# A warm-up on a tile that VectorE writes, and the first norm's weight column on GpSimd's queue

## The reference

```python
def rmsnorm(x, w):
    xf = x.astype(jnp.float32)
    y = xf * lax.rsqrt(jnp.mean(xf * xf, axis=-1, keepdims=True) + EPS)
    return (y * w.astype(jnp.float32)).astype(x.dtype)

h = rmsnorm(x, norm_mix_w[l])
proj = h @ w_in                      # 1024 -> hq, hf, hi, hgate, gq, gk, gv, ggate, glr
f = lb + (1.0 - lb) * jax.nn.sigmoid(hf.astype(f32))
...
x = x + token_mix(...)               # two gated recurrences and an output projection
x = x + cross_attend(...)            # attention into 256 memory tokens
x = x + moe(...)                     # top 4 of 32 experts, clamped SwiGLU
return rmsnorm(x, norm_final_w)
```

## Time and profile before

| what | value |
|---|---|
| median of 3 runs | 1188.06 us (1187.84 to 1188.17) |
| profiled execution | 1188.46 us |
| its span, from first to last instruction | 1186.7 us |
| TensorE busy | 1137.7 us, 96% of the span |
| VectorE, ScalarE, GpSimd busy | 32%, 15%, 2% |
| mean transfer rate | 375 GB/s, 444.89 MB |
| chain that ended last | PE 68%, DMA 30%, DVE 1% |

### The profile page before, as it was taken

The page is one execution under the profiler, slowest core; times in us unless marked ns, Lnnn a source line. Parts: engine busy times, 40 slices in busy tenths (PEclk is TensorE's granted clock), DMA queues, the critical chain, the costliest instruction groups (busy, mean ns, idle before and its releaser), DMA issues.

```text
span 1186.7 us, 18637 instructions
## 1 busy us (share of the span) xinstructions
PE 1137.7 (96%) x7483; PEld 572.1 (48%) x7484; DVE 379.4 (32%) x896; ACT 175.2 (15%) x366; POOL 19.0 (2%) x58
## 2 busy tenths in 40 slices
PE   9999999999999999999999999999999999999997
PEld 5988879855443443334333333333333333333332
DVE  4688878545222111122212121111111111111112
ACT  5311421243100000001000000000000000000002
POOL 3000010000000000000000000000000000000000
PEclk9999999999999999999999999999999999999999
DMA  9954203989999999999999999999999999999995
GB/s 306 380 196 144 73 10 120 350 334 383 420 426 434 430 429 432 426 436 429 435 430 430 435 428 436 430 434 430 433 432 429 436 428 436 429 434 423 426 424 222
DMA packets 42853, 444.89 MB, mean 375 GB/s; under 512 B 6308, under 2 KB 6772, under 8 KB 26040
## 3 DMA queue, kind: packets, MB, share of 16 engines
q1 hardware_dynamic: 41912, 441.63, 88.9%
q0 software_dynamic: 480, 1.85, 0.7%
q10 hardware_dynamic: 416, 0.79, 0.2%
HBM read 443.20 MB, written 1.05 MB: 374 GB/s over the span
## 4 chain that ended last, share of the span: by engine, by line
PE 68%; DMA 30%; DVE 1%; ACT 0%; SPq 0%; issue 0%; DVEq 0%; ACTq 0%
DMA ring<-in_w_gate_up 30%; PE bank L1168 23%; PE bank L1159 13%; PE bank L733 7%; PE bank L729 4%; PE bank L1198 4%; PE bank L1213 3%; PE bank L712 2%; PE bank L873 1%; PE bank L1095 1%; PE bank L1284 1%; PE bank L1189 1%; PE bank L1275 1%; PE bank L1007 1%; PE bank L1129 1%; PE bank L1087 1%
## 5 line engine op out<-in xcount | busy, mean ns | idle before, releaser
L1168 PE MATMUL bank<-ring,region 128*64 128x512 f32 x2048 | 464.2, 608 | 36.4 <-DMA ring<-in_w_gate_up 36.4
L1168 PEld LDWEIGHTS bank<-ring,region 128*64 128x64 f32 x2048 | 147.1, 140 | 333.9 <-issue 268.6
L1159 PE MATMUL bank<-ring,region 128*64 128x512 f32 x1024 | 226.8, 596 | 0.3 <-ACT region L1407 0.3
L2290 DVE TENSOR_SCALAR region<-bank 128x512 f32<-128x512 f32 x32 | 22.1, 692 | 570.4 <-PE bank L1168 570.4
L1159 PEld LDWEIGHTS bank<-ring,region 128*64 128x64 f32 x1024 | 71.2, 137 | 130.0 <-issue 127.2
L1407 ACT ACTIVATE region<-bank 128x256 f32<-128x256 f32 (+1 forms) x134 | 55.4, 440 | 369.0 <-PE bank L1159 251.0
L733 PE MATMUL bank<-ring 128*128 128x256 f32 x392 | 86.6, 381 | 0.0
L1407 ACT ACTIVATE bank<-region 128x512 f32<-128x512 f32 x32 | 19.2, 601 | 453.1 <-DVE region L2290 453.1
L733 PEld LDWEIGHTS bank<-ring 128*128 128x128 f32 x392 | 73.9, 190 | 10.9 <-issue 0.7
L1198 PE MATMUL bank<-region 64*128 64x512 f32 x264 | 65.6, 615 | 0.1
L1213 PEld LDWEIGHTS bank<-region,r_levels 128*128 128x128 bf16 x1536 | 61.2, 117 | 1.6 <-issue 1.6
(11 more groups left out here) (300 smaller groups left out, 761.4 us busy)
## 6 DMA issues: line engine op xcount, KB each, us to landing
ring<-in_w_gate_up SPq DMA_DIRECT2D x48, 4096.0 KB, 30.2
ring<-in_w_down SPq DMA_DIRECT2D x24, 4096.0 KB, 37.0
ring<-in_w_gate_up SPq DMA_DIRECT2D x26, 2048.0 KB, 15.2
ring<-in_w_down SPq DMA_DIRECT2D x10, 2048.0 KB, 14.3
ring<-in_w_in SPq DMA_DIRECT2D x6, 2048.0 KB, 17.3
ring<-in_w_gate_up SPq DMA_DIRECT2D x11, 1024.0 KB, 35.7
ring<-in_w_xkv SPq DMA_DIRECT2D x4, 2048.0 KB, 10.9
ring<-in_w_down SPq DMA_DIRECT2D x7, 1024.0 KB, 9.1
```

The costliest lines, as they stand in the source:

```text
L1159: last = pe.matmul(bk[half * ROWS:(half + 1) * ROWS, :], lhs, w[:, half * 512:(half + 1) * 512], start=start, stop=stop, skip_group_check= ...
L1168: last = pe.matmul(rows, lhs, columns[:, half], start=start, stop=stop, skip_group_check=True)
L2290: v.tensor_scalar(g_t, bank_g[:, :], LIMIT, None, ALU.min).then_inc(sem["g_clamped"], 1)
```

## The change

TensorE's warm-up reads a tile of ones, `warm` (the first 128 columns of a buffer that is free at that time), which VectorE writes as its first instruction; it signals warm_ready. There are seven matmuls instead of six, and one more, on the identity, stands behind the first flip of x. The wait for ident_ready moves behind the warm-up. The products of the first panel are in another order: tile 0's k 0 and 1, the flip of x's second tile, tile 0's k 2 and 3, tile 1's k 0 to 3, and then as before. The load of w_mix leaves SP's queue and is issued by POOL directly behind the identity. POOL's signal sums_ready is now a second count of consts_ready.

```diff
--- before.py
+++ after.py
@@ -83,7 +83,7 @@
 CUTS = 3
 MAXW = MAXB * E
 BY_TILE = [(E - 2, GU_CHUNKS - 1), (E - 1, GU_CHUNKS - 2), (E - 1, GU_CHUNKS - 1)]
-WARM_UP = 6
+WARM_UP = 7
 FIRST_ROWS = (0, 2, 4, 8)
 PAD = 32
 ROOT = D ** -0.5
@@ -135,7 +135,7 @@
         + ["xo00", "xo10", "eT00", "xo01", "eT01", "router0", "eT10", "xo11a", "xo11", "eT11", "router1"])
 
 SEMS = """quarter_joined rows_summed first_product seventh_product first_kept seventh_kept t1_ready t2_ready t3_ready t4_ready w_mix_in w_mem_in pads_zeroed glr_ready hT_scaled mem_in vec_in lb_in glr_in gk_bias_in router_in moe_row_in final_row_in down_bias_in gu_bias_in
- consts_ready sums_ready ident_ready masks_ready s_zeroed x_squared x_diag mem_squared mem_rms mem_scaled lb_diff lb_sigmoid f_ready lnf_ready
+ consts_ready warm_ready ident_ready masks_ready s_zeroed x_squared x_diag mem_squared mem_rms mem_scaled lb_diff lb_sigmoid f_ready lnf_ready
  z_abs z_ln g_ready hq_sigmoid r_diff r_exp r_ready gate_sigmoid gate_ready y_ready x1_squared
  neg_max p_ready x2_squared gu_part_ready gu_rest_ready router_scaled
  eT_part first_half_chosen half_used rank_psum h2T_part xw_ready cut_ready rest_ready panel_half scaled_ready rs_psum rs_ready gate_max gate_exps chosen_ready gates_ready heads_stat heads_mean
@@ -259,6 +259,7 @@
 
         xn = tm(region10)
         left_over = region10[:, D:2 * D]
+        warm = r_t[:, 0:P]
         norm_row = region2[:, 0:D]
         h2T = region10[:, 0:D].rearrange("p (k t) -> p k t", t=P)
         squares = r_t[:, 2 * D:3 * D]
@@ -437,7 +438,6 @@
                 return src.rearrange("(k p) n -> p k n", p=P)
 
             load_x(0)
-            sp.dma_start(w_mix, by_row(A["norm_mix_w"][0])).then_inc(sem["w_mix_in"], 16)
             load_x(1)
             for i in range(1, 3):
                 k = slice(FIRST_ROWS[i], FIRST_ROWS[i + 1])
@@ -584,6 +584,7 @@
             link(pool.memset(ident[:, :], 0.0))
             pool.affine_select(out=ident[:, :], in_=ident[:, :], compare_op=ALU.not_equal, fill=1.0, base=0,
                                pattern=[[-1, P]], channel_multiplier=1).then_inc(sem["ident_ready"], 1)
+            pool.dma_start(w_mix, A["norm_mix_w"][0].rearrange("(p k) -> p k", k=KT)).then_inc(sem["w_mix_in"], 16)
             pool.memset(gk2, 0.0).then_inc(sem["pads_zeroed"], 1)
             link(pool.memset(ones[:, :], 1.0))
 
@@ -612,7 +613,7 @@
             link(pool.memset(head_sum, 0.0))
             link(pool.memset(pair_sum, 0.0))
             link(pool.memset(head_sum[:, 0:1], 1.0))
-            pool.tensor_copy(pair_sum[:, 1:3], tri[:, CHUNK - 1::CHUNK]).then_inc(sem["sums_ready"], 1)
+            pool.tensor_copy(pair_sum[:, 1:3], tri[:, CHUNK - 1::CHUNK]).then_inc(sem["consts_ready"], 1)
 
             link(pool.memset(glr_padded, 0.0))
             pool.wait_ge(sem["glr_in"], 16 * (1 + P // PAD))
@@ -743,7 +744,7 @@
             def neighbours():
 
                 pe.wait_ge(sem["r_ready"], 1)
-                pe.wait_ge(sem["sums_ready"], 1)
+                pe.wait_ge(sem["consts_ready"], 2)
                 bk = begin("lv1")
                 for k in range(QT):
                     g = k % HEADS
@@ -851,9 +852,14 @@
                     end(last[half])
 
 
+            def keep_busy(tile, n):
+
+                for _ in range(n):
+                    pe.matmul(banks[7][:, 0:P], tile, tile, start=True, stop=True)
+
+            pe.wait_ge(sem["warm_ready"], 1)
+            keep_busy(warm, WARM_UP)
             pe.wait_ge(sem["ident_ready"], 1)
-            for n in range(WARM_UP):
-                pe.matmul(banks[7][:, 0:P], ident[:, :], ident[:, :], start=(n == 0), stop=(n == WARM_UP - 1))
             def flip_x(t):
 
                 pe.wait_ge(x_in[t], 16)
@@ -861,19 +867,28 @@
                     flip_by_row(f"xT{t}{h}", x_res, t, h)
 
             flip_x(0)
+            keep_busy(ident[:, :], 1)
             w, rows_bank = panel(0), [begin("hf0")]
-            for k0, k1 in zip(FIRST_ROWS, FIRST_ROWS[1:]):
-                pe.wait_ge(first_in[FIRST_ROWS.index(k0)], 16)
-                for t in range(NT):
-                    if (t, k0) == (1, 0):
-                        flip_x(1)
-                        rows_bank.append(begin("hf1"))
-                    for k in range(k0, k1):
-                        await_rows({0: [f"xT{t}0"], 4: [f"xT{t}1"]}, k)
-                        last = pe.matmul(rows_bank[t][:, :], hT[:, k, t * P:(t + 1) * P], w[:, k, :], start=(k == 0),
-                                         stop=(k == KT - 1))
-                    if k1 == KT:
-                        end(last, f"hf{t}")
+
+            def forget(t, k0, k1):
+
+                for k in range(k0, k1):
+                    await_rows({0: [f"xT{t}0"], 4: [f"xT{t}1"]}, k)
+                    last = pe.matmul(rows_bank[t][:, :], hT[:, k, t * P:(t + 1) * P], w[:, k, :], start=(k == 0), stop=(k == KT - 1))
+                if k1 == KT:
+                    end(last, f"hf{t}")
+
+            _, k1, k2, _ = FIRST_ROWS
+            pe.wait_ge(first_in[0], 16)
+            forget(0, 0, k1)
+            flip_x(1)
+            rows_bank.append(begin("hf1"))
+            pe.wait_ge(first_in[1], 16)
+            forget(0, k1, k2)
+            forget(1, 0, k2)
+            pe.wait_ge(first_in[2], 16)
+            for t in range(NT):
+                forget(t, k2, KT)
 
             pe.wait_ge(sem["glr_ready"], 1)
             bk = begin("glr")
@@ -1818,6 +1833,7 @@
                     weigh_half("xT", t, h, hT[:, 4 * h:4 * h + 4, t * P:(t + 1) * P], w_mix)
                 norm_diag(t, 0, sem["x_squared"], x_diag, sem["x_diag"])
 
+            v.memset(warm, 1.0).then_inc(sem["warm_ready"], 1)
             dve.wait_ge(sem["ident_ready"], 1)
             dve.wait_ge(sem["w_mix_in"], 16)
             for t in range(NT):
```

## The result

The changed kernel takes 1190.43 us (median of 18 runs, 1188.57 to 1195.81) against 1188.20 us of the kernel before (18 runs, 1187.73 to 1189.13): ratio 1.0020, 95% interval 1.0013 to 1.0027. It is slower by 2.2 us, and its times scatter over 7 us where those of before lie within 1.4. The forecast was 1188.0 us, 1187.1 to 1189.3. The execution of the changed kernel that was profiled took 1194.53 us (span 1192.8), one of the slowest of the 18; so its trace holds more of the loss than the median does. None of the 18 runs of before lies above 1189.13 us; in the runs of the same kernel beside the experiments some do (see "Open").

The account below looks back on a forecast made before the run. The expert weight stream bounds the second half, and start delays move it 1:1. First product at 6.95 plus 15.06 us puts glr at 22.01, 0.05 earlier: span 1186.65, median 1188.0 us, range 1187.1 to 1189.3.

Parts of the forecast that it names:

- the landing of the column: w_mix's load on GpSimd's queue: issued at 1.53 us, taking 3.6 us, landing near 5.1; bounds 3.8 and 7.0 us.
- quiet row: Profile row of GpSimd's transfers in a quiet stretch, 2.3 us, against 5.0 beside the weight stream; basis for the column's time.
- rival B: Late column: sharing with two full queues, it lands at 7.0 us, first product at 7.92; +0.9 us, 1189.0; chance 0.16.
- rival A: Quick start: panel part lands before 6.2 us, first product at 6.3 or 6.1; about 0.6 us gained, 1187.5; chance 0.27.
- The forecast's mechanism: At the start, x's second tile shares bandwidth with ScalarE's first panel part, which lands at 6.60 or 7.26 us; chance 0.52.
- C: Clock falls after TensorE idles 1.4 us or more at the start: 1.7 us on top, 1190.1 to 1190.7; chance 0.05.
- s: Start of TensorE's first product: 6.66 us before, forecast 6.95, between 6.66 and 7.32.
- The new order: First-tile products ahead of the second tile's cover TensorE's 0.34 us hole; 15.06 instead of 15.40 us to the glr product.
- The warm-up and the extra matmul: TensorE's start: warm-up begins near 1.1 us at no cost; extra matmul, at most 0.44 us, fits the 0.65 us hole.
- The 1:1 transmission: A microsecond won or lost before 26 us reaches 260 us whole and moves the expert weight stream and the end equally.

Follow-up runs that it names:

- e5: Changed kernel, but SyncE's and ScalarE's first loads wait until the weight column has landed; one timing, 1191.78 us.
- e1: Kernel before with only the weight column's load moved to GpSimd's queue behind the identity; 1191.44 us, ratio 1.0028.
- e3: Changed kernel with 12 instead of 1 idle matmuls behind the first flip; 1189.84 us, ratio 1.0013 to the kernel before.
- e7: Changed kernel with the weight column issued by ScalarE behind its panel part; 1190.19 us, ratio 1.0009.
- e6: Changed kernel with the weight column's issue ahead of the identity's memset on GpSimd; one timing, 1188.70 us.
- e8: Changed kernel with the weight column issued by ScalarE ahead of its panel part; 1190.55 us, ratio 1.0010.
- e10: Changed kernel, but SyncE issues x's second tile, and what stands behind it, only when the weight column has landed; one timing, 1188.22 us.
- e9: Changed kernel with each tile of x loaded as two transfers, in 2 KB instead of 4 KB rows; one timing, 1190.23 us.
- e2: Changed kernel with the weight column's load back between x's two tiles on SyncE's queue; 1187.65 us, ratio 1.0000 to the kernel before.
- e4: Kernel before with only the new order of the first products; 1188.28 us, ratio 0.9999.
- e11: Kernel before with only the new warm-up, seven matmuls on the tile VectorE writes; 1188.62 us, ratio 0.9999.

## Why the prediction was wrong, step by step

**The failed step is the landing of the column.** The prediction took "3.6 us, nearer the quiet row since it is small". It took 6.0, beyond even the 5.5 us that rival B allowed from the issue, and the issue itself came at 1.75 instead of 1.53 us. The quiet row was right about the path (1.9 us in e5) and useless for the place. The bounds came from GpSimd's rows, of 64 and 256 KB. Nearer rows were at hand: this very column had taken 4.48 us in the same rush, and with rival A's 0.4 us for the other path that gives a landing at 6.4 (an estimate), not "still before 5.5". The page of the kernel before also has the other three columns of 4 KB, all behind large loads in SyncE's queue:

```profile
norm_cols<-in_norm_mem_w SPq DMA_DIRECT2D x1, 4.0 KB, 7.3
norm_cols<-in_norm_moe_w SPq DMA_DIRECT2D x1, 4.0 KB, 11.1
norm_cols<-in_norm_xa_w SPq DMA_DIRECT2D x1, 4.0 KB, 10.2
```

What decides in these runs is what is queued when the column arrives. With x's second tile directly behind the first it took 5.8 to 6.2 us, issued at 1.75 by GpSimd (changed, e1, e3) or at 1.32 by ScalarE behind its panel part (e7). Issued ahead of the rush it was quicker beside the same tile: 5.1 us from 1.32 on GpSimd's queue (e6), 3.7 from 0.81 on ScalarE's (e8). With all that SyncE queues behind the first tile held back it took 3.9 (e10), with x in shorter rows 5.3 (e9). Its old place in SyncE's queue put it in front of the second tile, whose issue came 0.46 us later for it (1.72 instead of 1.26); that this was what made it quick is likely, not shown by itself.

**The forecast's mechanism was not at work.** That "those 420 KB now move beside 524 KB of x" was to delay the panel part to 6.60 or 7.26 us; it landed at 0.82 + 5.0 = 5.8. My reckoning of who had how many bytes left at 3.85 us rested on landings that all had the same 0.57 us behind their last byte, and that was not shown. e8 has the mechanism and more (landing 8.1), when the panel part is issued behind the column.

**Rival B was the right one, with too low a chance (0.16)**, and C came with it. B's own price was 0.9 us for a landing at 7.0; with 7.75 it is 2.01 at s. C's condition was an idle of 1.4 us and more, its price 1.7 us. The idle was 2.09 us, and the price in this trace follows from e2: there s to glr took 14.80 us, here 16.46, so 1.66. B and C were given as separate cases, but a late column is what makes the idle stretch. That was the error in the chances and in the range, which left C out. The median, 1190.43 us, lies in C's band of 1190.1 to 1190.7, but that is luck: C had a first product at 7.3 to 7.9 us and not at 8.67, and its condition, an idle of 1.4 us and more, was met in e7 (1.48 us) without a fall.

**The new order** was mis-sized: 0.34 us forecast, 0.60 measured from s to the glr product (e2; 0.62 in e4). The hole counts from the flip's modelled end to the next start. The starts alone go from 1.39 to 0.88 us, as the next product now starts 0.13 us ahead of that end; the other 0.09 lies in the 28 records behind it.

**The warm-up and the extra matmul**: nothing, as forecast (e11). TensorE began at 1.13 us, 1.1 forecast.

**The 1:1 transmission** held to 0.1 us as far as the first long weight wait, where the clock did not fall a second time: from the glr product to that wait ten traces have 549.41 to 549.53 us, for glr products between 21.5 and 26.1 us, and the three with the second fall 551.88 to 552.28. From that wait to the end of the span it is 1186.7 - 571.50 = 1115.2 us before and 1114.2 to 1115.8 in the others: within 1 us. So 1:1 holds to the end but for this scatter, which is larger than the forecast's whole gain or loss of 0.3 us.

**The median.** A start later by 2.01 us, less 0.60, would give +1.4 us. e3, with its clock at 1.00, gives +1.5 in the median, at a glr product 1.70 later. The changed kernel gives +2.2 and e1, without the gain of the order, +3.1, near the 3.2 of its trace. In the changed kernel's trace the first two parts alone come to 3.07 us, more than its median has. That the 0.7 us between +1.5 and +2.2 are clock falls at the start or near 280 us which not every run has is likely, not shown: of the 18 runs one was profiled.

**Open.** The exact rule by which the engines take turns: the panel part, with 2 KB rows, landed before x's second tile and the column behind it 1.6 us later (e7), which simple turns of one row each do not give. In the four traces with the column at 7.5 us or later it lands 0.2 to 0.4 us behind x's second tile, as if it waited for that tile; in e6 and e8 it lands well ahead of it. And why the clock falls near 280 us in some executions (changed, e4 and e11 of 13 traces): TensorE's work there is short pieces with small gaps around 279 us. Of 66 timings of the kernel before taken beside the experiments, 16 were above 1189.5 us. That these are such falls is likely from the sizes (2.4 to 2.8 us in three traces, whose executions were the longest or second longest of their kernels) but not shown, nor why none of the 18 runs of before in the result is so long.

## What to carry to other kernels

A small strided load was not made early here by a queue of its own, but by what did not yet stand in the other queues. If a few KB gate the first product, put them in front of the large load that can wait, price them by the nearest rows of the same shape and size, and read their landing from a trace with that traffic. And price an idle stretch of TensorE together with the clock that may fall behind it: here 2.0 us of waiting went with 1.7 us more of slow products. Filling the wait with idle matmuls took that back in the trace even though it overran by 0.6 us; in the timings 0.7 us of it show, and the intervals overlap.

## What the runs showed of the hardware

- A 4 KB column of 128 rows: 1.9 us from issue to landing alone (e5), 3.9 beside one tile of x and the panel part (e10), 5.8 to 6.2 with a second tile queued directly behind the first (changed, e1, e3, e7), 5.1 and 3.7 beside that tile when it was issued earlier (e6, e8).
- The clock at the start: behind idle stretches of 2.09, 2.36 and 2.13 us the granted clock fell to 1.2 GHz 0.9, 0.8 and 0.3 us into the next products (changed, e1, e8); behind 1.32 and 1.48 us it did not (e6, e7); in e9 it fell 0.1 us into them behind two shorter ones, 1.55 and 0.62 us, with the flips between. From s to the glr product these four took 16.46 to 16.79 us; e2, e3, e4, e6 and e7, with the same order of products as all but e1 and no fall, 14.72 to 14.80.
- The granted clock does not show every slow stretch: in e5, behind an idle stretch of 2.84 us, the same records took 0.92 us each and s to the glr product 16.59 us, with the granted clock at 1.00 throughout.
